# Two fused transformer blocks on one core: products over rows that make the next norm tile by tile, gates folded into weights, and attention with separate orders for scores and for values

## What is computed

```python
# block 1
h = modulate(rmsnorm(x, norm_mix_g), sh1, sc1)
o_a = g0 * o_cmp + g1 * o_sel + g2 * o_win          # softmax attention, 8 heads
o_b = stick_breaking(q, k, v)                       # a cumulative product along the keys
y   = sigmoid(m0) * (o_a @ w_proj_a) + sigmoid(m1) * (o_b @ w_proj_b)
x   = x + g1 * (y @ w_out)                          # "out1"
h   = modulate(rmsnorm(x, norm_ffn_g), sh2, sc2)    # "n2"
x   = x + g2 * ((silu(h @ w_gate) * (h @ w_up)) @ w_down)   # "up", "down"
x   = rmsnorm(x, norm_final_g)
# block 2
h   = rmsnorm(x, g_mix_2)                           # "n3", with the norm above
merged = sigmoid(a) * (y_a @ w_up_a) + sigmoid(b) * (y_b @ w_up_b)
x   = x + merged @ w_out_2                          # "out2"
h   = rmsnorm(x, g_ffn_2)                           # "n4"
x   = x + hier_moe(h, ...)                          # 32 experts, each with three matrices of 2 MB
x   = x + sigmoid(rmsnorm(x, g_ple) @ w_pg) * (p @ w_ple)
return rmsnorm(x, g_final)
```

## Time and profile before

| | us |
|---|---|
| median of 3 runs | 1971.08 (1970.47 to 1971.93) |
| the profiled execution | 1969.61 |
| its span, first to last instruction | 1967.9 |
| PE busy in the span | 1738.2 (88%) |
| DVE, ACT, POOL busy | 769.1, 515.8, 50.2 |

### The profile page before, as it was taken

The page is one execution under the profiler, slowest core; times in us unless marked ns, Lnnn a source line. Parts: engine busy times, 40 slices in busy tenths (PEclk is TensorE's granted clock), DMA queues, the critical chain, the costliest instruction groups (busy, mean ns, idle before and its releaser), DMA issues. The chain is left out here.

```text
span 1967.9 us, 20134 instructions
## 1 busy us (share of the span) xinstructions
PE 1738.2 (88%) x8167; PEld 1199.0 (61%) x8167; DVE 769.1 (39%) x1181; ACT 515.8 (26%) x820; POOL 50.2 (3%) x80
## 2 busy tenths in 40 slices
PE   2999979899979999999599989997999888898865
PEld 2887856546668888788488776665344333343354
DVE  4662555532352222333622453334233233232343
ACT  4212248722232222222332341322100000000032
POOL 0000000100000000000000000000200000000000
PEclk8999999989989999999799999998999999999987
DMA  9674050021412322220422011264799999999901
GB/s 352 217 267 132 1 192 1 1 81 52 167 43 89 125 86 86 89 104 8 153 86 86 24 63 43 86 257 164 292 428 424 426 427 427 427 427 427 405 1 43
DMA packets 86312, 354.73 MB, mean 180 GB/s; under 512 B 8734, under 2 KB 38090, under 8 KB 70346
## 3 DMA queue, kind: packets, MB, share of 16 engines
q1 hardware_dynamic: 83658, 345.03, 44.7%
q0 software_dynamic: 2560, 8.40, 1.1%
HBM read 343.93 MB, written 6.33 MB: 178 GB/s over the span
## 5 line engine op out<-in xcount | busy, mean ns | idle before, releaser
L539 DVE TENSOR_TENSOR p_w<-ring,p_w 128x1024 fp32r<-128x1024 f32 x68 | 83.3, 1225 | 173.3 <-ACT p_w L584 172.9
L544 PE MATMUL up_ps<-up_h,up_w 128*128 128x512 f32 x352 | 137.8, 391 | 5.7 <-DVE up_h L539 5.7
L545 PE MATMUL up_ps<-up_h,up_w 128*128 128x512 f32 x352 | 137.7, 391 | 0.0
L546 PE MATMUL up_ps<-up_h,up_w 128*128 128x512 f32 x352 | 137.5, 390 | 0.0
L2334 PE MATMUL ex_h<-s_ab,u_big_tail 128*64 128x512 f32 x400 | 116.2, 604 | 13.0 <-DMA s_ab<-in_w 5.7
L2334 PE MATMUL ex_h<-ring,u_big_tail 128*64 128x512 f32 x512 | 116.6, 603 | 11.6 <-DMA ring<-in_w 11.1
L584 ACT CAST p_w<-ring 128x1024 fp32r<-128x1024 f32 x68 | 71.3, 1048 | 128.4 <-PE p_ps L546 86.1
L2305 DVE TENSOR_TENSOR u_big_tail<-ex_x,vcol 128x512 f32<-128x512 f32 x32 | 20.6, 687 | 184.7 <-PE ex_x L2298 184.7
L2539 ACT ACTIVATE u_big_tail<-ex_h 128x512 f32<-128x512 f32 x16 | 9.6, 597 | 306.7 <-PE ex_h L2334 306.7
L539 DVE TENSOR_TENSOR up_w<-ring,up_w 128x1024 fp32r<-128x1024 f32 x44 | 53.9, 1226 | 87.3 <-ACT up_w L584 87.3
L2334 PEld LDWEIGHTS ex_h<-ring,u_big_tail 128*64 128x64 f32 x512 | 38.9, 138 | 75.0 <-issue 73.8
(11 more groups left out here) (501 smaller groups left out, 3519.4 us busy)
## 6 DMA issues: line engine op xcount, KB each, us to landing
ring<-in_w SPq DMA_DIRECT2D x48, 2048.0 KB, 28.7
s_ab<-in_w SPq DMA_DIRECT2D x36, 2048.0 KB, 28.3
ring<-in_w_in SPq DMA_DIRECT2D x19, 2048.0 KB, 7.9
ring<-in_w_ada SPq DMA_DIRECT2D x24, 1024.0 KB, 7.0
reg_a<-in_w SPq DMA_DIRECT2D x12, 2048.0 KB, 32.2
ring<-in_w_ffn_gate SPq DMA_DIRECT2D x11, 1024.0 KB, 5.2
ring<-in_w_ffn_up SPq DMA_DIRECT2D x11, 1024.0 KB, 7.7
ring<-in_w_ffn_down SPq DMA_DIRECT2D x5, 2048.0 KB, 7.8
```

Source lines behind the costliest of these rows:

```text
L539: return engine.tensor_tensor(lo, v, hi.bitcast(F32), ALU.subtract)
L544: nc.tensor.matmul(ps, x[0], y[0], start=start, stop=False)
L545: nc.tensor.matmul(ps, x[0], y[1], start=False, stop=False)
L546: return nc.tensor.matmul(ps, x[1], y[0], start=False, stop=stop)
```

## The change

- **Products over rows.** `stage_rows_out` now holds the norm behind it as well. The first step's operands are split in the stage before (`Steps`, `act_s`, `act_w`, `dve_gate`, `dve_s`, `dve_w` called from merge, up and hgrn). The gate row is multiplied into the weights, step by step, before they are split (`dve_gate`), so a finished bank needs one addition. The last three steps (out1) or two (down, out2) are taken bank by bank, in order of row tiles; each row tile is added, squared, scaled, transposed and split on its own; in out1 and out2 the transposes of tiles 0 and 1 stand between products. The scaled and shifted values are split straight into high and low parts. In down the two norms behind each other become one: z = x * row, squares of x and of z, and one root; `x` itself is scaled later, in project2. The first weight unit of up and project2 is split ahead too.
- **`Parts`** takes the operands that were made ahead (`made`), and skips its own splits of `hT` and of unit 0. All of it lives in one `arena`.
- **Attention.** Scores go in the old order (four sticks, then eight softs), transposes and values in another (stick, soft, soft for each pair of heads), five and six steps behind. Stick weights are made on DVE three steps behind the scores by that second order; DVE copies transposed stick units out of PSUM, ACT the soft ones. DVE multiplies by the spread factors straight from PSUM. `oa` is read where it lies, so its copy is gone, and the load of `h` into reg_a moves to the start of merge.
- **Router.** The normed rows are stored in four DMAs from out2, and the router waits for them one after the other.

```diff
-                i = at(s, 1)
-                if stick(i):
+                g = behind(s, LAG - 2)
+                if g is not None and stick(back[g]):
+                    weights(back[g])
+                g = behind(s, LAG)
+                if g is not None and stick(back[g]):
+                    k = (units[back[g]][0] + 1) * P
+                    dve.wait_ge(pt_ready, g + 1)
+                    if g >= 2:
+                        dve.wait_ge(pv, 2 * g - 2)
+                    nc.vector.tensor_copy(turned[g % 2][:, :, 0:k], ps_t[:, :, 0:k]).then_inc(copied_d, 1)
...
-            sp.dma_start(b.oa, b.early_oa).then_inc(oa_in, 16)
-            b.load_until(sp, b.c_merge1[1][0][0] + 1)
-            sp.wait_ge(oa_in, 16)
-            sp.dma_start(b.reg_a[:], b.h_dram).then_inc(b.h_back, 16)
...
+            sp.dma_start(b.reg_a[:], b.h_dram).then_inc(b.h_back, 16)
             sp.dma_start(b.x, x_load).then_inc(b.x_back, 16)
...
+    def dve_gate(self, dve, k):
+        _, c, kc, _ = self.steps[k]
+        self.b.wait_chunk(dve, c)
+        if self.gate_row is not None:
+            w = self.b.chunk(c)[:, kc, :]
+            self.nc.vector.tensor_tensor(w, w, self.gate_row[:], ALU.mult).then_inc(self.scaled, 1)
...
+            for t in range(NT):
+                for h in range(2):
+                    for k in range(begin, K):
+                        if t == 0 and h == 0:
+                            pe.wait_ge(st.lo, 2 * (k + 1))
+                        mm = st.products(ps[h * NT + t][:], k, t, h)
+                    mm.then_inc(ready, 1)
+                if t >= 2 and kind != "twice":
+                    turn(t - 2)
+            for t in range(0 if kind == "twice" else 2, NT):
+                turn(t)
...
-                    if gate_row is not None:
-                        if n >= 4:
-                            dve.wait_ge(ev, n - 3)
-                        nc.vector.tensor_tensor(tmp[:, n % 4], src, gate_row[:, cols], ALU.mult).then_inc(prod, 1)
```

More of the change, by code:

```diff
@@ L577, in act_w @@
     def act_w(self, act, u):
-        if u >= len(self.units):
+        if not self.made <= u < len(self.units):
             return
@@ L1055, in stage_attention @@
     N = len(units)
-    STEPS = N + 10
+    STEPS = N + LAG + 4
+    softs = [i for i in range(N) if units[i][2] < 2]
+    sticks = [i for i in range(N) if units[i][2] == 2]
+    back = [units.index((t, n, kind)) for t in order for n in range(4) for kind in (2, 0, 1)]
     def pair(reg, u0):
@@ new lines, in _ @@
+            square(0)
+            square(1)
+            normed(0)
+            square(2)
+            normed(1)
+            if kind != "twice":
+                split(0)
+            square(3)
+            normed(2)
+            if kind != "twice":
+                split(1)
+            normed(3)
+            for t in range(0 if kind == "twice" else 2, NT):
+                split(t)
+            if kind == "twice":
+                nc.scalar.activation(r1, ssx, ACT.Sqrt, scale=1.0 / D, bias=eps).then_inc(late, 1)
```

644 lines of the change are left out of this document (431 added, 213 removed).

## The result

The changed kernel takes **1940.46 us** (median of four runs, 1938.38 to 1943.10) where the kernel before takes 1970.78: a ratio of 0.9846, 95% interval 0.9829 to 0.9863, or 30.3 us less. The forecast was 1927, with a range of 1916 to 1940: the sign was right, the size too large by 13 us, and the time lies just outside the range. The profiled execution took 1938.65 us, its span is 1936.9.

What follows compares the result with a forecast made beforehand. TensorE was taken as the bound, waiting at stage starts, tails and attention, with the experts paced by their weights. Terms summed to -44.0 us from 1969.6, giving 1925.6, and 1927 for the median; range 1916 to 1940.

Steps and rivals of the forecast that it cites:

- The three rows: Up, project2, and from project2's end to out2's start: matmuls taken to stay as they are, forecast 0 us each.
- The starts: Starts of out1, down and out2: first step split in the stage before, PE starts 2.87 us earlier at each, -8.6 us.
- The clock at the starts: Starts of out1, down and out2: with waits of 1.7 us the half clock goes, -6.1 us; 0 if it comes anyway.
- Rival 1: Clock stays low at the starts, and longer at the heads of up and project2: costs 6.1 + 3, 1936 us; chance 0.13.
- Behind out1: From out1's last product to up's first: norm, shift and split laid out per row tile, 14.9 against 19.94 us, -5.0.
- rival 2: Tails of out1 and down bound by DVE, 0.29 us for each small operation: about +7 us, 1934; chance 0.13.
- Behind down: From down's last product to project2's first: two norms as one, 15.6 against 28.67 us, -13.1.
- Attention: Attention: DVE keeps up with the sticks and PE waits less, -6 us (4 to 5 of fill, 1 at the end).
- rival 3: Attention gives nothing, PE waiting for DVE's copies at stick units, or h loads slowly: +6 to +9 us, 1935; chance 0.12.
- The load of h: Merge's start: PE waits behind DVE for the moved load, 7.5 us on a free queue: +1.3 us.
- Rival 4: Preparing a step (gate, high, low) paces PE in all 38 steps: slower than before, 1988 us at 7.0 each; chance 0.02.
- Rival 5: Experts do not start earlier in effect, fewer weights loaded ahead: some 13 us come back, 1940 us; chance 0.03.

Runs made afterwards that it cites:

- aligned: The changed kernel with small tensors and padding put ahead of reg_a, so that h_high and the arena lie 92,160 bytes apart: 1931.79 us, ratio 0.9790.

## Why the prediction came out as it did

**The step that failed** is in its first paragraph: "All other matmuls stay as they are." The change gives the operands of up, project2 and the mixed stage new places, and I had read this as free. The three rows hold 12.2 us; 9 to 10 of them are the places (8.2 in up and project2, which come back when the operands are moved, and 0.6 to 2.1 in the stage behind), and the rest are the 0.5 us wait and the half clock told above. None of the five rivals named it. It could have been seen that every product over h gets a high part from another region than its other operands; that this has a price no row of the trace before shows, since all its operands lay alike. The undo (aligned) and the do-alone (32 and 64 bytes in the kernel before) both show it, so this cause is shown. What in the memory makes it so is not.

The Trainium skill ("TensorE: Matmul & The Clock Gate", section "Step-by-step: what each phase is for") says that TensorE reads its streaming operand and its next weights through two ports of their own, so that loading weights takes nothing from the running product. The page gives no reason there for which the operands' places should matter. 863 products for 884 in the same 200 us say that, in this kernel, they do.

**The starts** (-8.6) are as forecast to 0.1 us, but they were not free: the splits ahead of down make PE wait 0.5 us inside up, a term that the prediction put at nothing ("DVE and ACT have room there").

**The clock at the starts** (-6.1) as well: 5.9, and 5.4 came back when the waits did. Rival 1 falls for the starts. It was partly right about the heads: up's first 3.8 us still run at half clock, as 3.6 us did before:

```profile
556.90:570.60 13.70, 5.73 (x17) 4.61 (x18) 9.32 (x23) 4.67 (x6) 0.00 (x0) 0.50 0.00 1
```

**Behind out1** (-5.0, measured -3.5) the mis-sized term is "a split is 3.1, three are 9.4". DVE's timeline and its group with ACT's in this stretch:

```profile
552.78 2.63 DVE L1658 TENSOR_SCALAR s_ab<-out_ps,mulcol,modcol 128x128 f32<-128x128 f32 x8
...
557.24 2.62 DVE L1658 TENSOR_SCALAR s_ab<-out_ps,mulcol,modcol 128x128 f32<-128x128 f32 x8
...
561.23 2.64 DVE L1658 TENSOR_SCALAR s_ab<-out_ps,mulcol,modcol 128x128 f32<-128x128 f32 x8
```

```profile
L1727 ACT CAST h_high<-s_ab 128x512 fp32r<-128x512 f32 x6 | 3.6, 615 | 3.5 <-DVE s_ab L1658 3.4
```

Eight in 2.63 us are 0.33 us each, where I took 0.23, and rival 2 had 0.29. The 0.23 did not follow from its own premise: 1024 columns take DVE 1.23 us and 512 take 0.69 (the low parts of two sizes), so 384 columns fewer than 512 save 0.4 of the 0.7 and leave 0.3, and of the 0.745 that rival 2 starts from 0.34. Three splits take from 552.78 to 565.31, 12.5 us for 9.4; other waits came out 1.6 us shorter. Rival 2's mechanism, in size 3.1 us and not 7, is real in this one tail. Behind down a small operation takes DVE 0.26 us (32 in 8.36), and there it matters less:

```profile
L1670 DVE SCALAR_TENSOR_TENSOR arena<-down_ps,vcol,h_high 128x128 fp32r<-128x128 f32 x32 | 8.4, 342 | 0.1
```

(its mean of 342 ns counts overlap between operations; the total over 32 is what the tail pays.) The 0.26 us that the prediction worked out from the Trainium skill ("VectorE: DVE Perf Modes", section on the TRN2 errata) is what the trace shows for this form; for the form with two columns of factors it is too low.

**Behind down** (-13.1, measured -13.4) and **behind out2** (-6.5, measured -6.5) held, the first as a sum: its 32 small operations took 8.4 us for the forecast 7.4, and what stood beside them 1.3 less.

**Attention** (-6.0, measured -4.5): the waits fell about as forecast, by 6.9 us in the profiled execution, and 2.4 us of that were lost again to the clock in the last row tile. The forecast had no term for a clock there. Where the waits fell is right at the two ends (the fill: 7.0 us on L1214 before, now 1.3 for DVE's first copy and 1.1 in shorter waits; the last wait 4.1, now 3.2). In between two things that the forecast had left out of its sum nearly cancel: waits on ACT fell from 9.1 to 3.7 us, and at the three changes of row tile PE now waits 5.2 us in all for DVE, 3.0 of them with its copy of the transposed sticks as releaser, the place that rival 3 had named.

**The load of h** (+1.3, measured +1.6): the chain was right to the engine: load, then ACT, DVE, and PE behind DVE's eviction. It landed after 7.9 us instead of 7.5:

```profile
reg_a<-h_saved SPq DMA_DIRECT2D x1, 2048.0 KB, 7.9
```

The agreement is partly luck. The prediction's own terms (7.5, 1.05, 1.22 and 0.69) add up to 10.5 us and not 10.7, and the wait goes with the clock and the load: with projections at full clock it is 3.7 us, with the load landing after 9.0 us (aligned kernel) 2.1.

**Rival 4** (preparation paces PE) has nothing for it: down keeps 487 products in 110 us. **Rival 5** neither: from the experts' first product to the end of the span it is 586.35 us before and 586.25 after.

**The range** was too narrow above. It allowed for known terms mis-sized, and held nothing for a stage that I had declared untouched while its operands were moved.

## What to carry to other kernels

Where a change moves operands of TensorE, ask how far apart they now lie, and compare the number of matmuls in an equally long, fully busy stretch: busy time and the granted clock look the same when every product is 2% slower. Here a distance that is a multiple of 256 bytes between the operands' starts gave the full pace, and moving one region by 1,888 bytes gave 11 us; 96 bytes gave the same pace in their one trace. A wait for a load should stand directly ahead of the first instruction that needs it, not at the head of an engine's program: what is queued behind it includes evictions for which TensorE waits. And the same stretch of short TensorE work ran at full clock in three traces and at half in seven; a term for it belongs in the range.

## What the runs showed of the hardware

- The pace of back-to-back 512-column products depends on the distance between operands in a partition. Multiples of 256 bytes: 226 to 227 ns (distances 92,160, 93,696, 93,952, and all of before). 94,048 bytes: 230 to 233 ns by line. 94,016 bytes: 230 to 238 ns in up. The clock was 1.00 in all. It holds across products too: with 24,416 bytes between the operands of products that alternate it was 231 ns, with 22,528 it was 226.7. Where the weights stream and h is held (project2's first half) it is 231 ns at 94,048.
- After a wait of 1.7 us TensorE went on at clock 1.00 at three starts; after waits of 4.8 to 5.4 us at 0.50, for another 3.1 to 5.0 us.
- A 128-column operation out of PSUM took DVE 0.26 us with one column of factors and 0.33 with two, ACT 0.26 with a scale (32 in 8.36 us) and 0.37 with scale and shift.
